# A two-block transformer kernel: another order of loads, norms and copies in the first stage and in the attentions

## The reference

```
def rmsnorm(x, g):
    y = x32 * lax.rsqrt(jnp.mean(x32 * x32, axis=-1, keepdims=True) + RMS_EPS)
    return (y * g.astype(jnp.float32)).astype(x.dtype)

def memory_attention(qm, mem_n, w_mem_kv):      # mem_n = rmsnorm(mem, g_mem), 256 memory tokens
    mk, mv = jnp.split(mem_n @ w_mem_kv, 2, axis=-1)
    s = einsum("bshd,bmhd->bhsm", q4, mk) * (MEM_DH ** -0.5)      # 4 heads of 128
    return einsum("bhsm,bmhd->bshd", softmax(s), mv)

# first block
h = rmsnorm(x, g_pre_mix); proj = h @ w_in
(cb, cc, cv, q, k, v, qm, ga, gb, gc) = split(proj)
y_a = conv branch; y_b = causal attention, 8 heads of 64, with a relative bias; y_c = memory attention
x = x + rmsnorm((gates * branches) @ w_out, g_post_mix)
x = x + rmsnorm((gelu(a) * g) @ w_down, g_post_ffn)      # a, g from a convolution over rmsnorm(x) @ w_up
```

## Time and profile before

| | |
|---|---|
| median of 3 runs | 1674.34 us (1672.49 to 1677.17) |
| the profiled execution's own time | 1672.39 us |
| its span in the trace | 1670.6 us |
| TensorE busy | 1581.7 us, 95% |
| VectorE busy | 910.8 us, 55% |
| ScalarE busy | 621.8 us, 37% |

### The profile page before, as it was taken

One profiled execution on the slowest core, in us unless ns is written; L12 is line 12 of the kernel. 1 busy time (PEld: TensorE's weight loads), 2 busy tenths in 40 slices (PEclk: granted clock), 3 DMA queues, 4 the chain that ended last, 5 costly groups with the idle time before them and its releaser, 6 DMA issues.

```text
span 1670.6 us, 20770 instructions
## 1 busy us (share of the span) xinstructions
PE 1581.7 (95%) x7854; PEld 1323.5 (79%) x7854; DVE 910.8 (55%) x1472; ACT 621.8 (37%) x865; POOL 11.8 (1%) x16
## 2 busy tenths in 40 slices
PE   5899998999998999999999789898999999999999
PEld 5788777888877788888888658897887788888887
DVE  6344465644553777777423767877655444444322
ACT  6241333333233444444323445364454333223211
POOL 0000000000000000000000000000000000000000
PEclk9999999999999899999999999888999999999999
DMA  6312221222222122222423212101102222222222
GB/s 230 139 38 101 73 73 51 98 78 100 100 91 86 51 101 100 100 100 75 151 100 109 87 46 101 51 26 51 52 26 76 76 100 100 100 100 99 103 101 75
DMA packets 24746, 147.05 MB, mean 88 GB/s; under 512 B 2499, under 2 KB 4931, under 8 KB 8172
## 3 DMA queue, kind: packets, MB, share of 16 engines
q1 hardware_dynamic: 24684, 146.21, 24.7%
HBM read 144.07 MB, written 2.13 MB: 88 GB/s over the span
## 4 chain that ended last, share of the span: by engine, by line
PE 81%; DVE 10%; ACT 5%; issue 3%; DMA 0%; DVEq 0%; ACTq 0%; SPq 0%
PE bank L1605 24%; PE bank L1607 24%; PE bank L1606 24%; ACT w_hi L550 2%; PE bank L1699 2%; PE bank L1717 2%; DVE w_lo L989 2%; PE bank L1984 1%; PE bank L1923 1%; PE bank L1706 1%; DVE sel L1382 1%; DVE st L1381 1%; DVE w_lo L997 1%; DVE row L1119 1%; PE bank L1658 0%
## 5 line engine op out<-in xcount | busy, mean ns | idle before, releaser
L1605 PE MATMUL bank<-h_hi,w_hi 128*128 128x512 f32 (+1 forms) x1200 | 475.1, 396 | 12.1 <-DVE h_lo L1058 10.3
L989 DVE TENSOR_TENSOR w_lo<-raw,w_hi 128x2048 fp32r<-128x2048 f32 x119 | 272.6, 2291 | 392.3 <-ACT w_hi L550 391.6
L1607 PE MATMUL bank<-h_hi,w_lo 128*128 128x512 f32 (+1 forms) x1200 | 468.8, 391 | 0.0
L1606 PE MATMUL bank<-h_lo,w_hi 128*128 128x512 f32 (+1 forms) x1200 | 468.6, 390 | 0.0
L550 ACT ACTIVATE w_hi<-raw 128x2048 fp32r<-128x2048 f32 x129 | 246.4, 1910 | 353.9 <-PE bank L1607 351.6
L1605 PEld LDWEIGHTS bank<-h_hi,w_hi 128*128 128x128 f32 (+1 forms) x1200 | 225.3, 188 | 65.5 <-DVE h_lo L1058 9.9
L1607 PEld LDWEIGHTS bank<-h_hi,w_lo 128*128 128x128 f32 (+1 forms) x1200 | 225.3, 188 | 48.7
L1606 PEld LDWEIGHTS bank<-h_lo,w_hi 128*128 128x128 f32 (+1 forms) x1200 | 225.5, 188 | 47.6 <-issue 1.0
L1605 PE MATMUL bank<-a_hi,w_hi 128*128 128x512 f32 x352 | 136.9, 389 | 0.0
L1606 PE MATMUL bank<-a_lo,w_hi 128*128 128x512 f32 x352 | 136.9, 389 | 0.0
L1607 PE MATMUL bank<-a_hi,w_lo 128*128 128x512 f32 x352 | 136.9, 389 | 0.0
(11 more groups left out here) (265 smaller groups left out, 1969.4 us busy)
## 6 DMA issues: line engine op xcount, KB each, us to landing
raw<-weights SPq DMA_DIRECT2D x129, 1024.0 KB, 4.8
toep<-bias_scratch SPq DMA_DIRECT2D x8, 448.0 KB, 4.6
x<-xT SPq DMA_DIRECT2D x1, 2048.0 KB, 14.8
outT<-x SPq DMA_DIRECT2D x8, 256.0 KB, 4.3
memT<-memT SPq DMA_DIRECT2D x1, 1024.0 KB, 5.9
mem2T<-mem2T SPq DMA_DIRECT2D x1, 1024.0 KB, 5.6
masks_in<-masks SPq DMA_DIRECT2D x1, 512.0 KB, 3.1
vec<-vec SPq DMA_DIRECT2D x1, 140.5 KB, 5.7
```

The costliest lines, as they stand in the source:

```text
L989: nc.vector.tensor_tensor(w_lo[m % 2][:, :], raw[m % 2][:, :], w_hi[m % 2][:, :].bitcast(F32), ALU.subtract).then_inc(lo_ready, 1)
L1605: nc.tensor.matmul(o, lh, rh, start=first, stop=False)
L1606: nc.tensor.matmul(o, lh, rl, start=False, stop=False)
L1607: return nc.tensor.matmul(o, ll, rh, start=False, stop=last)
```

## The change

- Two more inputs: the memory and x with the tokens on the partitions (mem_tok, 1 MB, and x_tok, 2 MB). ScalarE squares a row of 1024 features and sums it in the same instruction, two for the memory, four for x. `squares`, `add_squares` and `norm_sum` are no longer used for these two norms.
- The first loads: vec goes first; memT and load 0 are cut into halves that alternate (memT 0, load 0 first half, memT 1, load 0 second half, load 1), then mem_tok, xT, ident, onehot, rel_bias; load 2 follows once the low part of load 0 is made; then x_tok, then load 3 and the rest. ScalarE and VectorE round and split load 0 by halves.
- ScalarE takes a square root of a constant before anything else.
- TensorE makes the first two key tiles side by side, feature tile by feature tile, beginning with the first half of load 0. The memory's spread comes after the first value tile, x's spread between the two qm loads.
- VectorE reads the mk tiles in the order 2, 3, 0, 1, and makes the low part of load 6 between the second and third qm tile.
- In every attention ScalarE's copy of the transposed exponentials comes before the step's exponential.

```diff
-            sp.dma_start(memT[:, :, :], A["memT"].rearrange("(k p) t -> p k t", p=P)).then_inc(mem_in, 16)
+            def mem_half(c):
+                half = slice(c * KT // 2, (c + 1) * KT // 2)
+                sp.dma_start(memT[:, half, :], A["memT"].rearrange("(k p) t -> p k t", p=P)[:, half, :]
+                             ).then_inc(mem_in[c], 16)
             sp.dma_start(vec[:, :], A["vec"]).then_inc(vec_in, 16)
-            load(0)
+            mem_half(0)
+            sp.dma_start(raw[0][:, 0:SLOT // 2], A["weights"][0, :, 0:SLOT // 2]).then_inc(raw_half, 16)
+            mem_half(1)
+            sp.dma_start(raw[0][:, SLOT // 2:SLOT], A["weights"][0, :, SLOT // 2:SLOT]).then_inc(raw_full[0], 16)
             load(1)
+            sp.dma_start(mem_tok[:, :, :], A["mem_tok"].rearrange("(t p) d -> p t d", p=P)).then_inc(mem_tok_in, 16)
             sp.dma_start(x[:, :, :], A["xT"].rearrange("(k p) t -> p k t", p=P)).then_inc(x_in, 16)
...
-            stream(2, FIRST["v"] + 2)
+            sp.wait_ge(lo_ready, 1)
+            load(2)
+            sp.dma_start(x_tok[:, :, :], A["x_tok"].rearrange("(t p) d -> p t d", p=P)).then_inc(x_tok_in, 16)
+            stream(3, FIRST["v"] + 2)
```

ScalarE, in the attention and in the first stage:

```diff
                 for s in range(count + LAG):
+                    if s >= LAG:
+                        ...
+                        frees(("T", w), nc.scalar.activation(tb[...], B(("T", w))..., ACT.Copy))
                     if s < count:
                         ...
-                    if s >= LAG:
-                        ...
-                        frees(("T", w), nc.scalar.activation(tb[...], B(("T", w))..., ACT.Copy))
...
+            act.wait_ge(set_up, 1)
+            nc.scalar.activation(st[:, 4, 15:16], ones[:, 0:1], ACT.Sqrt)
             act.wait_ge(vec_in, 16)
+            act.wait_ge(mem_in[0], 16)
             for j in range(KT):
+                if j == KT // 2:
+                    act.wait_ge(mem_in[1], 16)
                 raised(mn_hi[:, j, :], memT[:, j, :], "g_mem", j)
-                squares(memT[:, j, :])
                 if j == 1:
-                    round_w(0)
+                    act.wait_ge(raw_half, 16)
+                    nc.scalar.activation(w_hi[0][:, 0:SLOT // 2], raw[0][:, 0:SLOT // 2], ACT.Copy).then_inc(hi_half, 1)
+                if j == KT // 2:
+                    act.wait_ge(raw_full[0], 16)
+                    nc.scalar.activation(w_hi[0][:, SLOT // 2:SLOT], raw[0][:, SLOT // 2:SLOT], ACT.Copy
+                                         ).then_inc(hi_ready, 1)
+            def token_squares(src, count, first):
+                for t in range(count):
+                    ins = nc.scalar.activation(src[:, t, :], src[:, t, :], ACT.Square,
+                                               accum_out=st[:, 4, first + t:first + t + 1])
+                ins.then_inc(tok_sums, 1)
             round_w(1)
+            act.wait_ge(mem_tok_in, 16)
+            token_squares(mem_tok, MT, 8)
             act.wait_ge(x_in, 16)
             for j in range(KT):
                 raised(h_hi[:, j, :], x[:, j, :], "g_pre_mix", j)
-                squares(x[:, j, :])
-                if j == 2:
+                if j == 1:
+                    root(MT, mean_ready, 1)
                     round_w(2)
                 if j == 5:
+                    keep_rms("mem", rms_mem, M)
                     round_w(3)
-                if j == 6:
-                    norm_root("mem", M)
+            act.wait_ge(x_tok_in, 16)
+            token_squares(x_tok, TT, 10)
             round_w(4)
-            keep_rms("mem", rms_mem, M)
             act.wait_ge(rms_col, 1)
             ...                                  # the four mv copies
+            root(TT, mean_ready, 2)
             round_w(FIRST["qm"] + 1)
+            keep_rms("x", rms)
             round_w(FIRST["qm"] + 2)
-            norm_root("x", S)
             ...                                  # the two bias copies
-            keep_rms("x", rms)
```

VectorE:

```diff
+            def token_norm(tokens, first, keep):
+                count = tokens // P
+                dve.wait_ge(tok_sums, 1 + keep_of.index(keep))
+                nc.vector.tensor_scalar(st[:, 0, 0:count], st[:, 4, first:first + count], 1.0 / D, EPS, ALU.mult, ALU.add
+                                        ).then_inc(mean_ready, 1)
+                inverse_root(count)
+                nc.vector.tensor_copy(st[:, 5, keep:keep + count], st[:, 2, 0:count]).then_inc(rms_col, 1)
+                for c in range(count):
+                    ins = nc.vector.tensor_scalar(diag[:, c, :], ident[:, :], st[:, 2, c:c + 1], None, ALU.mult)
+                ins.then_inc(diag_ready, 1)
...
             split_w(1)
             dve.wait_ge(const_in, 16)
+            token_norm(M, 8, 8)
             for j in range(KT):
                 low_gained(h_lo[:, j, :], x[:, j, :], "g_pre_mix", h_hi[:, j, :], j)
-                add_squares(j == 0)
-                if j == 2:
+                if j == 1:
                     split_w(2)
                 if j == 5:
-                    norm_scale("mem", M, keep=8)
                     split_w(3)
                     ...                          # the four mk products, now tiles 2, 3, 0, 1
             split_w(4)
+            token_norm(S, 10, 0)
             split_w(5)
-            split_w(6)
-            norm_scale("x", S, keep=0)
             wait_free(("spread", "x"))
             for t in range(4):
                 ready(("qm", t))
                 normal("qm", t, qm[:, t, :])
+                if t == 1:
+                    split_w(6)
             split_w(FIRST["v"] + 1)
```

TensorE:

```diff
+            pe.wait_ge(lo_half, 1)
+            for kt in range(KT):
+                if kt == KT // 2:
+                    weights(0)
+                pe.wait_ge(split, kt + 1)
+                for c in range(2):
+                    ...                          # product of feature tile kt into mem_k tile c
+            weights(1)
+            ...                                  # mem_k tiles 2 and 3
             pe.wait_ge(set_up, 2)
-            norm_sum("mem", M, (ssq_mem, M))
             for m in range(2):
-                if m == 1:
-                    norm_spread("mem", M)
                 weights(2 + m)
                 for t in range(MT):
                     ...
+                    if m + t == 0:
+                        norm_spread("mem", M)
-            feature_loads("qm", 2, fresh=LOW_END["mem"])
-            norm_sum("x", S)
+            for m in range(2):
+                ...                              # the same qm products
+                if m == 0:
+                    norm_spread("x")
             ...                                  # the bias matmuls
-            norm_spread("x")
```

More of the change, by code:

```diff
@@ L104 @@
     LOW_END[_name] = _at
-NORM_SUMS = {"mem": 8, "x": 16, "mix": 24, "ffn": 32, "down": 48, "x_2": 56, "ffn_2": 68}
+NORM_SUMS = {"mix": 8, "ffn": 16, "down": 32, "x_2": 40, "ffn_2": 52}
 IW_SCALE = IDXH ** -0.5 * 64 ** -0.5
@@ L168, in plan_banks @@
     tiles("mem_k", 4, first=0, per=2)
-    norm("mem")
     tiles("mem_v", 4, (4, 5, 2, 3), first=2, per=2)
+    use(("spread", "mem"), 6)
     tiles("qm", 4, first=FIRST["qm"], per=2)
+    use(("spread", "x"), 6)
     tiles("bias", 2, (4, 5))
-    norm("x")
     attention("mem", MHEADS * TT)
@@ L283, in build @@
         mn_lo = at("mn_lo", AR + 80 * K, [KT, M], F32R)
+        mem_tok = at("mem_tok", AR, [MT, D])
+        x_tok = at("x_tok", AR + 32 * K, [TT, D])
         qm = at("qm", AR + 48 * K, [4, S])
@@ L367, in build @@
         bank_free = [sem(f"bank_free{b}") for b in range(8)]
-        mem_in, x_in, vec_in, const_in, onehot_in = (sem(x_) for x_ in ("mem_in", "x_in", "vec_in", "const_in",
-                                                                        "onehot_in"))
+        mem_in = [sem("mem_in0"), sem("mem_in1")]
+        raw_half, hi_half, lo_half = sem("raw_half"), sem("hi_half"), sem("lo_half")
+        mem_tok_in, x_tok_in, tok_sums, mean_ready = (sem(x_) for x_ in ("mem_tok_in", "x_tok_in", "tok_sums",
+                                                                         "mean_ready"))
+        x_in, vec_in, const_in, onehot_in = (sem(x_) for x_ in ("x_in", "vec_in", "const_in", "onehot_in"))
         mem2_in, mask_in = sem("mem2_in"), sem("mask_in")
@@ L591, in attention @@
                 for s in range(count + LAG):
+                    if s >= LAG:
+                        w = UNIT0[kind] + s - LAG
+                        keys = UNITS[w][3]
+                        ready(("T", w))
+                        if w >= 2:
+                            ready(("O", w - 2))
+                        frees(("T", w), nc.scalar.activation(
+                            tb[w % 2][:, 0:keys // P, :], B(("T", w))[:, 0:keys].rearrange("p (c t) -> p c t", t=P),
+                            ACT.Copy))
                     if s < count:
@@ L1143, in _ @@
                 low_gained(mn_lo[:, j, :], memT[:, j, :], "g_mem", mn_hi[:, j, :], j)
```

(52 more changed lines are left out.)

2 lines of the change are left out of this document (1 added, 1 removed).

## The result

The changed kernel takes 1659.03 us, median of 4 runs (1657.84 to 1660.11), against 1675.34 before in the same set: 16.3 us less. The ratio is 0.9904, 95% interval 0.9891 to 0.9917. The forecast was 1655, range 1647 to 1666. One execution of one kernel further down (whole first loads) took 3188.06 us, twice its others; why is open, and no figure here uses it.

What follows compares the result with a forecast made beforehand. TensorE, busy 95% of the span, was taken to bound the kernel, so only its standing time and lower clock could yield. From 1674.34, 7.2 (first stage) and 11.7 (copy) off gave 1655 us, range 1647 to 1666.

Steps and rivals of the forecast that it cites:

- The sum: Whole kernel: 7.2 us from the first stage and 11.7 from the copy, giving 1655 us.
- the copy: Attention loops: with ScalarE's copy before the exponential, TensorE's transposes wait less; 11.7 us won, bounds 0 and 17.7.
- the first stage: Everything before the first scores: 5.7 us from earlier scores plus 1.5 from the clock, 7.2 us, bounds 1 and 9.
- The start: First loads: smaller transfers land sooner and are rounded by halves, so TensorE begins at 9.0 instead of 14.07 us.
- a full queue: Load queue: 1 MB takes about 2.45 us when the queue is full, used for all landing times.
- The stop: TensorE before load 2's products: waits from 22.7 to 27.4, then the lower clock costs 1.5 us.
- The tail: Between the last qm products and first scores: sum, spread, rms and three qm products leave; scores at 70.2 instead of 75.86.
- the cover of three steps: First attention steps: VectorE's late maximum is needed only three steps later; without that cover up to 4 us lost.
- B: Attention loops, rival: the copies' waits return at the O bank or S; gain only 2 to 3 us, 1664.6; chance 0.13.
- D: Attention loops, rival: exp(s) waits for the transpose in each of 80 steps, 28 us slower, 1695; chance 0.03.
- C: First stage, rival: 3 MB more before loads 2 and 3 and four squares push qm to 51; 1661.3; chance 0.12.
- fixed cost for each transfer: Load queue: 2.0 us plus bytes over 436 GB/s per transfer; three added transfers would cost 6 us, sum about 1661.

Runs made afterwards that it cites:

- whole first loads: The changed kernel with memT and load 0 each as one transfer again: median 1653.75 us, ratio to before 0.9879.
- the other order: The changed kernel with ScalarE rounding load 3 before the memory's rms copy, and x_tok's four squares behind load 4's rounding: 1653.05 us, ratio 0.9879.
- the copy alone: The kernel before, with only ScalarE's copy of the transposed exponentials put before the step's exponential in all attentions: 1663.28 us, ratio 0.9938.
- the first stage alone: The changed kernel with the old order in the attentions, exponential before copy: 1668.49 us, ratio 0.9967.
- both edits: The changed kernel with memT and load 0 whole, load 3's rounding ahead of the rms copy, four squares behind load 4's rounding: 1654.64 us, ratio 0.9876.

## Why the prediction was right, and where it was off

**The sum.** Forecast 18.9 us, measured 16.3. By parts: the copy 11.7 forecast, 11.1 measured; the first stage 7.2 forecast, 5.9 measured. In the first stage two errors go against each other: the scores come 4.1 us earlier where I had 5.7, and the clock gives 2.0 where I had 1.5. The interval is about 2 us wide on either side, so only the trace says what was off.

**The start.** First matmul at 9.0 forecast, 9.88 measured. The first half of memT landed at 5.3 (1.2 + 4.1), as forecast, though that figure doesn't follow from my own sum (7.0 less 1.4 is 5.6); the table load went under it. But the second half landed 7.6 us after its issue at 2.2, at 9.8, where I had taken 8.1 from a full queue. "1 MB takes about 2.45 us in a full queue, and I use that throughout" is the step that failed: it does not hold for half memT, and everything behind it came late, load 1 at 13.6 instead of 11.9, x at 22.2 instead of 20.2, load 2 at 25.1 instead of 23.3. Of load 2's 1.8 us the halves of memT make about 1.3, by the experiment.

**Load 2 and the clock.** The stop was forecast from 22.7 to 27.4 with the lower clock behind it; it ran from 23.94 to 29.47. The mechanism was right, the size off by the late landing. From there the forecast's chain holds step by step, 1.7 to 2.1 us late: ScalarE keeps rms at 34.9, rounds load 3, the second half of the values begins at 39.88 instead of 37.8, and the four squares push load 4's low part to this place on VectorE:

```profile
44.29 2.29 DVE L1023 TENSOR_TENSOR w_lo<-raw,w_hi 128x2048 fp32r<-128x2048 f32 x1 [2.24 <-ACT w_hi L566]
```

It ends at 46.6 instead of 44.9, and qm began at 47.19 instead of 45.2. I took the second half of the values from a warm TensorE; the clock fell there once more (7.3 us for values that take 5.8). But without that fall they would have ended at 45.6, ahead of the low part, and qm would still have begun near 46.9 (an estimate: the low part's end and the 0.3 us that I had behind it). So of the 2.0 us some 0.3 are this clock's and 1.7 came down from the landings: the term that was mis-sized is load 2's landing. The forecast names ScalarE's steps on this way but not what their order costs: with the other order load 2's products begin no earlier (29.84) and qm 3.6 us earlier.

**The tail.** Its own length was right: 2.1 us from the end of the qm products to the scores forecast, 1.9 found (69.9 to 71.79), the clock kept up. The long way back of spread, rms and qm products was worth 4.5 us by the experiment. VectorE's next maximum came at 76.52, 2 us after my figure; it cost TensorE 0.24 us at the fourth step, so the cover of three steps was just long enough.

**The copy.** The case-by-case reading held: 14.2 us of 17.7 gone, 4.6 back at the output bank, net 9.6, and by landmarks 0.4, 4.3 and 6.0 of time against 0.75, 5.0 and 5.9 forecast. The 1.1 us by which the landmarks exceed the waits isn't assigned. One sign that I had set was missed: the wait for o_tok and mix was to grow by no more than 3, and it grew by 4.6, from 2.6 to 7.2; it stays under the 10 that I had called wrong. In the second block the first wait shrank from 4.69 to 3.02, by 1.7.

**The rivals.** B (waits come back in full) and D (slower) fell with the copy alone, C (no gain in the first stage) with the first stage alone. The reading of the Trainium skill's fixed cost for each transfer (page DMA: Bandwidth & Descriptors) as a rival was worth its place: undivided, memT saved 1.3 us, not the 2.0 us of that fit, and the halves of a weight load cost nothing measurable. The page has that fit for transfers issued by GpSimd, and all of these go through SyncE's queue, so it is not the fit itself that was tested here but my use of it. Neither that use nor my row alone was right.

## What to carry to other kernels

In an engine's queue, put the instruction whose input is ready ahead of the one that waits for a slow partner, and then look what the freed engine waits for next; that second wait kept a third of what the first had cost. Whether the same turn helps on the neighbouring engine depends on where in the step its input is made: it paid on ScalarE, and on VectorE it brought nothing and probably cost time. An early start that only leads to a longer stop is a loss where the stop lowers the clock: judge a stage by the last thing that leaves it, here qm's start and the first scores.

## What the runs showed of the hardware

The time of one kernel moves with TensorE's clock in stages that the change does not touch. Windows 470:490 and 900:945, of the kernel with both edits and then of the one with whole first loads:

```profile
470.00:490.00 20.00, 17.54 (x72) 14.11 (x71) 12.06 (x18) 6.47 (x10) 0.00 (x0) 0.91 0.29 103
900.00:945.00 45.00, 36.85 (x189) 30.65 (x189) 31.41 (x47) 21.00 (x28) 2.85 (x2) 0.89 0.31 107
```

```profile
470.00:490.00 20.00, 17.54 (x77) 14.20 (x77) 13.05 (x19) 7.04 (x10) 0.00 (x0) 1.00 0.31 106
900.00:945.00 45.00, 36.65 (x197) 30.84 (x196) 33.62 (x51) 20.48 (x28) 2.85 (x2) 0.96 0.29 105
```

The programs are the same there. The first has its scores 2.4 us earlier (65.89 against 68.25) and ends 4.4 us later (spans 1653.5 and 1649.1). What makes the clock fall in one execution and not in the other is open; it was not isolated. It is why differences of 2 us between these kernels are read from the trace's landmarks and not from the times.
